# Order of the products in the feed-forward groups of a two-layer decoder trunk: low parts first, four column blocks ahead of both down products

## The reference, cut to what matters

```python
D_MODEL, SEQ, DEPTH, D_FF = 1024, 256, 2, 2816

def swiglu(t, w_gate, w_up, w_down):
    return (jax.nn.silu(t @ w_gate) * (t @ w_up)) @ w_down

for l in range(DEPTH):
    x = x + 0.5 * swiglu(rmsnorm(x, ffn1_norm[l]), ffn1_w_gate[l], ffn1_w_up[l], ffn1_w_down[l])
    x = x + mixing(x)          # latent attention and sliding-window attention, not touched here
    x = x + 0.5 * swiglu(rmsnorm(x, ffn2_norm[l]), ffn2_w_gate[l], ffn2_w_up[l], ffn2_w_down[l])
```

## Time and profile before

| | before |
|---|---|
| median of 3 runs (lowest to highest) | 937.29 us (937.19 to 937.37) |
| profiled execution, first to last instruction | 935.2 us |
| PE busy | 922.3 us (99%) |
| PE weight loads busy | 784.0 us (84%) |
| DVE, ACT busy | 624.9 us (67%), 533.6 us (57%) |
| read from HBM | 163.86 MB, 176 GB/s over the span |

### The profile page before, as it was taken

How to read it: one execution, slowest core, us unless ns; L and a number is a source line. 1 busy time by engine, 2 the same in 40 slices (tenths; PEclk the granted TensorE clock), 3 DMA queues, 4 the chain that set the end, 5 groups by cost and what they waited for, 6 DMA issues and landing times.

```text
span 935.2 us, 14752 instructions
## 1 busy us (share of the span) xinstructions
PE 922.3 (99%) x4970; PEld 784.0 (84%) x4970; DVE 624.9 (67%) x937; ACT 533.6 (57%) x1034; POOL 74.6 (8%) x159
## 2 busy tenths in 40 slices
PE   7999999999999999999999999999999999999998
PEld 5888888888788888888888888888887888888887
DVE  5766666685887666666676666666858776666663
ACT  7655554566875555554555555555669565555551
POOL 3000000023320000000020000000342100000000
PEclk9999999999999999999999999999999999999999
DMA  7855555551064755555556555555501566555541
GB/s 290 267 184 191 191 185 196 179 184 65 23 223 156 250 183 190 192 189 193 180 160 239 197 183 189 193 189 175 199 1 65 199 207 207 194 185 193 188 157 46
DMA packets 45814, 165.43 MB, mean 177 GB/s; under 512 B 5296, under 2 KB 5296, under 8 KB 45776
## 3 DMA queue, kind: packets, MB, share of 16 engines
q1 hardware_dynamic: 44496, 160.98, 50.2%
q0 software_dynamic: 992, 3.42, 1.2%
q10 hardware_dynamic: 288, 0.54, 0.1%
HBM read 163.86 MB, written 1.05 MB: 176 GB/s over the span
## 4 chain that ended last, share of the span: by engine, by line
PE 92%; DVE 3%; ACT 2%; issue 1%; DMA 1%; DVEq 1%; POOL 0%; SPq 0%; POOLq 0%
PE UV L1379 31%; PE UV L1386 16%; PE A L1316 12%; PE A L1319 11%; PE A L1320 11%; PE UV L1316 2%; PE UV L1320 2%; PE UV L1319 2%; PE UV L1641 1%; PE UV L1331 1%; ACT work L791 1%; DMA raw<-stream 1%; DVE wlo L905 1%; PE UV L1622 1%; PE A L1608 0%
## 5 line engine op out<-in xcount | busy, mean ns | idle before, releaser
L905 DVE TENSOR_TENSOR wlo<-raw,whi 128x1024 fp32r<-128x1024 f32 x304 | 370.5, 1224 | 127.8 <-ACT whi L555 127.3
L555 ACT ACTIVATE whi<-raw 128x1024 fp32r<-128x1024 f32 x304 | 317.0, 1051 | 11.2 <-DMA raw<-stream 11.0
L1379 PE MATMUL UV<-acts,whi 128*128 128x512 f32 x1280 | 318.8, 391 | 0.0
L1379 PEld LDWEIGHTS UV<-acts,whi 128*128 128x128 f32 x1280 | 234.9, 188 | 46.8 <-DVE wlo L905 1.5
L1386 PEld LDWEIGHTS UV<-acts,wlo 128*128 128x128 f32 x1280 | 174.3, 190 | 12.1
L1386 PE MATMUL UV<-acts,wlo 128*128 128x256 f32 x1280 | 178.8, 283 | 0.0
L1316 PE MATMUL A<-whi,ht_hi 128*128 128x512 f32 x352 | 138.2, 392 | 0.0
L1319 PE MATMUL A<-wlo,ht_hi 128*128 128x512 f32 x352 | 137.9, 392 | 0.0
L1320 PE MATMUL A<-whi,ht_lo 128*128 128x512 f32 x352 | 137.0, 389 | 0.0
L630 ACT ACTIVATE ht_hi<-work 128x256 fp32r<-128x256 f32 x80 | 33.4, 418 | 121.9 <-DVE work L996 121.9
L626 ACT ACTIVATE work<-UV 128x256 f32<-128x256 f32 x80 | 30.7, 384 | 88.8 <-PE UV L1386 88.6
(11 more groups left out here) (217 smaller groups left out, 849.6 us busy)
## 6 DMA issues: line engine op xcount, KB each, us to landing
raw<-stream SPq DMA_DIRECT2D x304, 512.0 KB, 3.3
gain<-norm_gains POOLq DMA_DIRECT2D x5, 512.0 KB, 5.7
out<-x SPq DMA_DIRECT2D x4, 256.0 KB, 2.1
sgain<-small_gains POOLq DMA_DIRECT2D x2, 324.0 KB, 4.1
x<-x_in SPq DMA_DIRECT2D x1, 512.0 KB, 3.6
x<-x_in ACTq DMA_DIRECT2D x1, 512.0 KB, 7.5
cs<-rope POOLq DMA_DIRECT2D x1, 128.0 KB, 5.4
cgain<-col_gains POOLq DMA_DIRECT2D x2, 1.0 KB, 4.2
```

The lines of the kernel that those rows point to most:

```text
L555: act.activation(whi_half(unit, half), raw[:, n % RAW, :], ACT.Copy).then_inc(hi_done, 1)
L905: dve.tensor_tensor(wlo_half(unit, half), raw[:, n % RAW, :], whi_half(unit, half).bitcast(F32), ALU.subtract).then_inc(split_done, 1)
L1379: last = pe.matmul(UV[c][:, j, :], whi_half(unit, j)[:, k * P:(k + 1) * P], acts[:, :, k, :], start=k == 0, stop=False, skip_group_check=True)
```

## The change

A column block now begins with the narrows (low weights) and ends with the wides; the matmuls are the same, and the first narrow starts the bank. In `ffn_step`, all four blocks of a group come ahead of both down products. PE waits for the split h of the previous group's second half ahead of the third block. At the end of each group's down product of c = 0 PE counts a new semaphore, `low_phase`, and ACT's copy of the fourth block's up half waits for it, up to group 9. On ACT and DVE the work on that half (copy, sum, product, high and low part) moves to the head of the next group's list, the gate work of c = 1 moves ahead of its first split, and the last splits follow one another. The order in which units are handed back, and the slots of h's parts (`wide_h`), follow.

```diff
@@ units_in_freed_order
-                order += [at + 3 * g, at + 3 * g - 1, at + 3 * g + 1]
+                order += [at + 3 * g] + ([at + 2, at + 4] if g == 1 else [at + 3 * g + 1, at + 3 * g - 1])
@@
+        low_phase = sem("low_phase")
...
+        def late_no(l, f, g, i=0):
+
+            return i + ((l * 2 + f) * (NG - 2) + g)
+
         def wide_h(g, c):
 
-            at = 2 if g == NG - 1 and c == 1 else c
+            at = c * (1 + g % 2)
@@ ACT
             def up_copy(l, f, g, c, i=0):
                 act.wait_ge(block_done, 2 * sub_no(l, f, g, c, i))
+                if c == 1 and g < NG - 1:
+                    act.wait_ge(low_phase, late_no(l, f, g, i))
                 act.activation(up_b, UV[c][:, 1, SEQ:512], ACT.Copy).then_inc(up_copied, 1)
...
             def ffn_group(l, f, g, i=0):
 
                 at = l * LU + FFN_AT[f] + 3 * g
+                if g > 1:
+                    up_copy(l, f, g - 1, 1, i)
+                    h_high(l, f, g - 1, 1, i)
                 gate_copy(l, f, g, 0, i)
                 split(at + 3, 0, i)
                 silu_wide(l, f, g, 0, i)
                 up_copy(l, f, g, 0, i)
                 split(at + 3, 1, i)
                 h_high(l, f, g, 0, i)
+                gate_copy(l, f, g, 1, i)
                 split(at + 4, 0, i)
-                gate_copy(l, f, g, 1, i)
+                silu_wide(l, f, g, 1, i)
                 split(at + 4, 1, i)
-                silu_wide(l, f, g, 1, i)
-                up_copy(l, f, g, 1, i)
                 split(at + 5, 0, i)
-                h_high(l, f, g, 1, i)
                 split(at + 5, 1, i)
 
             def last_group(l, f):
...
+                up_copy(l, f, g - 1, 1)
+                h_high(l, f, g - 1, 1)
                 gate_copy(l, f, g, 0)
@@ DVE
             def ffn_group(l, f, g, i=0):
 
                 at = l * LU + FFN_AT[f] + 3 * g
+                if g > 1:
+                    up_sum(l, f, g - 1, 1, i)
+                    wide_product(l, f, g - 1, 1, i)
+                    h_low(l, f, g - 1, 1, i)
                 gate_sum(l, f, g, 0, i)
                 split(at + 3, 0, i)
                 up_sum(l, f, g, 0, i)
+                wide_product(l, f, g, 0, i)
                 split(at + 3, 1, i)
-                wide_product(l, f, g, 0, i)
                 h_low(l, f, g, 0, i)
+                gate_sum(l, f, g, 1, i)
                 split(at + 4, 0, i)
-                gate_sum(l, f, g, 1, i)
                 split(at + 4, 1, i)
-                up_sum(l, f, g, 1, i)
                 split(at + 5, 0, i)
-                wide_product(l, f, g, 1, i)
-                h_low(l, f, g, 1, i)
                 split(at + 5, 1, i)
 
             def last_group(l, f):
...
+                up_sum(l, f, g - 1, 1)
+                wide_product(l, f, g - 1, 1)
+                h_low(l, f, g - 1, 1)
                 gate_sum(l, f, g, 0)
@@ PE
                 half_split(unit, j, i)
                 for k in range(KD):
-                    last = pe.matmul(UV[c][:, j, :], whi_half(unit, j)[:, k * P:(k + 1) * P], acts[:, :, k, :],
-                                     start=k == 0, stop=False, skip_group_check=True)
+                    low = pe.matmul(UV[c][:, j, 0:SEQ], wlo_half(unit, j)[:, k * P:(k + 1) * P], act_hi[:, :, k, :],
+                                    start=k == 0, stop=False, skip_group_check=True)
                     if k == 0 and freed:
-                        last.then_inc(unit_freed, freed)
+                        low.then_inc(unit_freed, freed)
                 if amid:
                     amid()
                 for k in range(KD):
-                    last = pe.matmul(UV[c][:, j, 0:SEQ], wlo_half(unit, j)[:, k * P:(k + 1) * P], act_hi[:, :, k, :],
+                    last = pe.matmul(UV[c][:, j, :], whi_half(unit, j)[:, k * P:(k + 1) * P], acts[:, :, k, :],
                                      start=False, stop=k == KD - 1, skip_group_check=True)
                 last.then_inc(block_done, 1)
@@ down
+                if 1 <= g < NG - 1 and c == 0 and t == 1:
+                    last.then_inc(low_phase, 1)
 
             def ffn_step(l, f, g, i=0):
 
                 columns(l, f, g, 0, 0, i)
                 columns(l, f, g, 0, 1, i)
+                pe.wait_ge(h_w_split, sub_no(l, f, g - 1, 1, i))
+                columns(l, f, g, 1, 0, i, freed=1)
+                columns(l, f, g, 1, 1, i)
                 down(l, f, g - 1, 1, 0, i, freed=1)
                 down(l, f, g - 1, 1, 1, i)
-                columns(l, f, g, 1, 0, i, freed=1)
-                columns(l, f, g, 1, 1, i)
                 down(l, f, g, 0, 0, i, freed=1)
                 down(l, f, g, 0, 1, i)
```

## The result

| | before | changed |
|---|---|---|
| median (lowest to highest), 21 runs each | 937.36 us (936.80 to 938.63) | 939.12 us (938.49 to 941.39) |
| ratio to before, 95% interval | | 1.0019, 1.0013 to 1.0025 |
| profiled execution, span | 935.2 us | 937.2 us |

The change costs 1.8 us. That is clear of zero, and at 0.19% just under the line of 0.2% that the prediction took for "no change"; the interval, 0.13% to 0.25%, reaches past that line.

What follows compares the result with a forecast made beforehand. PE's own pace was taken to bound the kernel. Four first blocks losing 0.45 us each add 1.8 us, all other parts 0: 937.29 + 1.8 = 939.1 us, range 937.7 to 940.3.

Steps and rivals of the forecast that it cites:

- The first block: First column block of each FFN: PE waits for h at its transposition, 0.45 us lost, four times, 1.8 us.
- the restart: PE going on after its wait for h: second wide behind the transpositions 0.57 us after h, against 0.45 undisturbed after the transpositions.
- rival of dearer waits: Transposition in the first blocks and last down product: each FFN loses 0.53 us, 2.1 us in all, 939.4; chance 0.33.
- the slow stretch behind the narrows: Each run of narrows is followed by about 0.03 us of slow 512-column matmuls, in either order.
- Low parts first in the other blocks: Column blocks: 160 runs of narrows either way, a block stays 2.79 us; cost 0.
- Four blocks ahead of both downs, held read: Group loop: group stays 16.61 us, PE's added wait before the third block has 2.6 us of room; cost 0, gain 0.
- The backlog on DVE: DVE's last two splits run 1.1 us into the next group; the held block's chain is done by 3.0 us.
- Reads of PSUM: Wides in the group loop: reads don't slow them, so moving reads gains 0; the opposite rival, 935.6 or 935.2, chance 0.07.
- The sign that the prediction asked for: Profile after: eight wides of every block at 1.84 us although no read falls among them.
- The end of the FFN: Last down product, waiting for the last block's h: room shrinks from 0.05 to 0.02 us; cost 0, at worst 0.03 each.
- a held read that is late: Rival at the third block: PE waits in 9 groups per FFN, 0.1 us each is 3.6 us, 940.9; chance 0.08.
- the 4.3 to 4.8 us of slow wides: Rival that reads slow wides: 160 x 0.03 in play, about 3.5 gained less 1.8 lost, 935.6, or 935.2; chance 0.07.

Runs made afterwards that it cites:

- h_sooner: Changed kernel with DVE's product of h for the second row tile of group 0 ahead of group 1's second weight split: 937.35 us, ratio 0.9998 to the kernel before.
- first_wide: Changed kernel with the eight wides first again in the first column block of each FFN only: 937.43 us, ratio 0.9998 to the kernel before.
- first_narrow: Kernel before with narrows first in the first column block of each FFN, nothing else: 939.42 us, ratio 1.0023 to the kernel before.
- low_first_rest: Kernel before with narrows first in the 39 other blocks of each FFN: 937.24 us, ratio 0.9999 to the kernel before.
- order_only: Changed kernel with wides first in every block, its group order, ACT and DVE lists and held read kept: 937.12 us, ratio 1.0000 to the kernel before.
- reads_twice: Kernel before with ACT's copies of a half out of PSUM taken twice in 38 of 40 blocks per FFN: 937.34 us, ratio 0.9998 to the kernel before.

## Why the prediction was right, point by point

**Forecast.** 939.1 us forecast, 939.12 measured; the profiled span was to be 937.0 and was 937.2, of which 0.19 came ahead of the change. That the median agrees to 0.02 us is luck: single runs spread over 2.9 us.

**The first block.** The sum said: h 1.41 us after the first matmul, narrows through at 1.06, second wide behind the transposition at 301.47 - 299.49 = 1.98, 0.45 lost net. Measured in the changed kernel: h at 301.55 - 300.14 = 1.41. The second wide and those behind it, in the changed kernel:

```profile
302.12 1.78 PE L1400 MATMUL UV<-acts,whi 128*128 128x512 f32 x7
```

and in h_sooner:

```profile
300.92 1.75 PE L1400 MATMUL UV<-acts,whi 128*128 128x512 f32 x7
```

In the changed kernel the second wide starts 302.12 - 300.14 = 1.98 after the first matmul and 0.57 after h: the row for a wait of the same instruction, gave the restart rightly. Without the wait it starts at 300.92 - 299.38 = 1.54, where the sum had 1.51, so the wait itself costs 0.44 here and not 0.47. The gap from first matmul to first down matmul is 0.48 longer than in the kernel before; there the slow stretch behind the narrows, 0.03, fell on the down product behind the block, now it lies within the block. That leaves 0.45, and the table of starts has 0.43 to 0.48 per FFN. The rival of dearer waits needed 0.53 and falls. That this one place makes the loss is shown by first_wide, first_narrow and h_sooner, each of which moves the whole of it.

**Low parts first in the other blocks: 0.** low_first_rest has a ratio of 0.9999.

**Four blocks ahead of both downs, held read: 0.** order_only has a ratio of 1.0000, and the group of the changed kernel is 16.61 us long. The backlog on DVE was as worked out: its two splits end at 110.25 + 2.36 = 112.61, 1.16 us into the group (1.1 forecast); the low part of the held h is done at 113.89 + 0.43 = 114.32, 2.87 us into it (3.0 forecast), and the third block starts at 117.03, 2.7 us later. No wait of PE stands there.

**Reads of PSUM.** Two rows of the kernel before, had to carry this against the coincidence in the earlier trace rows. They were thin: of ACT's read at 32.15 only 0.21 us lies before the wides end at 32.36. The conclusion held all the same: reads doubled (reads_twice) change nothing, and reads moved away (low_first_rest) leave 1.84 us and the time as it was. The sign that the prediction asked for, 1.84 us with no read among the wides, is clean only in low_first_rest; in the changed kernel DVE's sum of the held half still starts at 112.53, among the wides from 112.40. The Trainium skill, "PSUM — Partial Sum Buffer", section "PSUM bank collisions raise a hardware error", which the prediction draws on, says that the hardware does not stall when two engines meet on a bank. The reads here are of a bank that PE isn't writing, and these runs show no stall for them either.

**The end of the FFN.** In the changed kernel's first FFN h's last low part and the first weight load of the last down product, answering to the earlier trace rows:

```profile
191.06 0.43 DVE L1011 TENSOR_TENSOR ht_lo<-work,ht_hi 128x256 fp32r<-128x256 f32 x1 [0.48 <-ACT ht_hi L637]
...
191.57 0.19 PEld L1330 LDWEIGHTS A<-whi,ht_hi 128*128 128x128 f32 x1
```

191.57 - 191.49 = 0.08 us, where 0.11 was before. Of the 0.05 to spare 0.02 is left, as forecast, and nothing was lost.

**What the prediction was loose on.** It gave the rival of dearer waits 0.33 on a difference of 0.3 us, which no run here could have told from the forecast by its time alone; the rows could. And the earlier trace rows proves less than it was used for: a stretch cut to one group's length is always that long. The group's length is the difference of two starts, 16.61 us in both kernels. Two sums of its rivals don't come out: 3.6 us for a held read that is late gives 942.7 with the 1.8 of the forecast and 940.9 only without it, and all of the 4.3 to 4.8 us of slow wides gained, less 1.8, gives 934.3 to 934.8 and not 935.2. Neither bears on the forecast.

## What to carry to other kernels

When runs of a PE-bound loop are put in another order, look for a step of another engine that was timed to fall under the longer run: here a transposition had 0.54 us of room under eight wides and lacked 0.35 under eight narrows, and one line in DVE's list decides it. Slow matmuls beside a read are no proof that the read slows them; find a place in the same trace where the two come apart, then double the read. Where a short run is followed by a slow stretch, count the runs, not the matmuls.

## What the runs showed of the hardware

A run of 256-column matmuls of this 4-byte format that goes straight over into 512-column ones is followed by about 0.03 us of slow ones, whatever reads PSUM meanwhile: 1.84 us for eight where 1.81 is usual, in the kernel before, in the changed one and in reads_twice. Putting runs together takes it away in part: 16.61 us a group with four runs of eight, 16.57 with two of 16, 16.55 with one of 32.

Such a run isn't the only thing that the stretch stands behind, and behind a transposition it can be missing. Seven wides at 0.227 take 1.59 us. Behind the standstill at the head of the second FFN's first block, with no narrows ahead, seven take 301.44 - 299.83 = 1.61 in the kernel before:

```profile
299.83 1.77 PE L1379 MATMUL UV<-acts,whi 128*128 128x512 f32 x7
```

In h_sooner PE waits for h in none of the four first blocks. The eight wides behind narrows and transpositions take 302.50 - 300.60 = 1.90 in the second FFN, but 762.97 - 761.04 = 1.93 in the fourth:

```profile
761.04 2.09 PE L1400 MATMUL UV<-acts,whi 128*128 128x512 f32 x8
...
762.97 0.39 PE L1330 MATMUL A<-whi,ht_hi 128*128 128x512 f32 x1
```

What makes the stretch wasn't tried and stays open.
